# Expert layers begun from the first token tile alone, and the top-k of a head moved by half a step

## What is computed

```python
x <- LN(alpha * x + gate1 * mixer(x * (1 + scale1) + shift1))
x <- LN(alpha * x + gate2 * PEER(x * (1 + scale2) + shift2))
```

```python
q = (t @ wq).astype(f32).reshape(T, PEER_HEADS, PEER_DK)
s1 = jnp.einsum('thd,hkd->thk', q[..., :half], k1.astype(f32))
s2 = jnp.einsum('thd,hkd->thk', q[..., half:], k2.astype(f32))
v1, i1 = lax.top_k(s1, PEER_TOPK)
v2, i2 = lax.top_k(s2, PEER_TOPK)
...
top_s, pos = lax.top_k(cand_s, PEER_TOPK)
idx = jnp.take_along_axis(cand_i, pos, axis=-1)
gate = jax.nn.softmax(top_s, axis=-1)
...
act = jax.nn.gelu(jnp.einsum('td,thkd->thk', tb, u_tab[ib]).astype(f32), approximate=False)
return jnp.einsum('thk,thkd->td', (gb * act).astype(tb.dtype), v_tab[ib])
```

## Time and profile before

| what | value |
|---|---|
| median of 3 runs | 2070.34 us (2067.26 to 2072.97) |
| profiled execution | 2069.5 us |
| its span | 2067.7 us |
| TensorE busy | 1739.6 us, 84% |
| VectorE busy | 1502.9 us, 73% |
| ScalarE busy | 597.6 us, 29% |
| q0, all gathers | 536.90 MB |
| mean granted TensorE clock | 0.948 |
| gathers | 475.9 to 2038.5 us, 512 of them |

### The profile page before, as it was taken

One profiled execution on the slowest core, in us unless ns is written; L12 is line 12 of the kernel. 1 busy time (PEld: TensorE's weight loads), 2 busy tenths in 40 slices (PEclk: granted clock), 3 DMA queues, 4 the chain that ended last, 5 costly groups with the idle time before them and its releaser, 6 DMA issues.

```text
span 2067.7 us, 17872 instructions
## 1 busy us (share of the span) xinstructions
PE 1739.6 (84%) x5310; PEld 973.9 (47%) x5310; DVE 1502.9 (73%) x3506; ACT 597.6 (29%) x1415; POOL 484.1 (23%) x516
## 2 busy tenths in 40 slices
PE   5998988978899877889998899977998888777776
PEld 5777467765444332334343478654454333222222
DVE  6899986657676767888786676566767776877765
ACT  3554651512232223323232121002222222222221
POOL 0000000003333333333333000003333333333331
PEclk9999998989999999999999899988999999999999
DMA  8244216638999999899999774429999999999996
GB/s 326 89 155 144 82 62 242 248 126 348 419 420 419 420 412 417 351 402 391 383 420 380 290 295 178 167 91 419 420 420 420 417 413 412 394 419 420 420 419 258
DMA packets 94472, 668.11 MB, mean 323 GB/s; under 512 B 11271, under 2 KB 11560, under 8 KB 14504
## 3 DMA queue, kind: packets, MB, share of 16 engines
q0 software_dynamic: 73728, 536.90, 63.2%
q1 hardware_dynamic: 20648, 130.08, 16.6%
HBM read 665.82 MB, written 1.11 MB: 323 GB/s over the span
## 4 chain that ended last, share of the span: by engine, by line
PE 39%; DMA 29%; DVE 13%; issue 2%; ACT 2%; PEldq 0%; POOL 0%; PEld 0%; DVEq 0%; SPq 0%; POOLq 0%; ACTq 0%
DMA expert_rows<-in_p_uv,chosen_experts 28%; PE bank L898 21%; PE bank L965 4%; DVE dot_products L1875 4%; PE bank L864 4%; PE bank L829 2%; PE bank L808 2%; PE bank L1040 1%; PE bank L1005 1%; PE bank L994 1%; ACT weight_diagonal L1272 1%; DVE modulation_products L1395 1%; PE bank L927 1%; PE bank L915 1%; DVE scores L1839 1%
## 5 line engine op out<-in xcount | busy, mean ns | idle before, releaser
L898 PE MATMUL bank<-expert_rows,weight_diagonal 128*128 128x512 f32 x2048 | 985.0, 626 | 200.0 <-ACT weight_diagonal L1272 199.9
L1875 DVE SCALAR_TENSOR_TENSOR dot_products<-expert_rows,bank 128x1024 f32<-128x1024 f32 x512 | 624.9, 1220 | 338.3 <-DMA expert_rows<-in_p_uv,chosen_experts 332.4
L1061 POOL DMA_INDIRECT expert_rows<-in_p_uv,chosen_experts x512 | 483.9, 945 | 1555.2 <-PE bank L898 823.5
L898 PEld LDWEIGHTS bank<-expert_rows,weight_diagonal 128*128 128x128 f32 x2048 | 393.6, 198 | 730.2 <-issue 406.4
L1263 ACT ACTIVATE expert_gelu<-expert_dots 128x2 f32<-128x2 f32 x256 | 52.1, 203 | 723.2 <-DVE dot_products L1875 722.8
L1272 ACT ACTIVATE weight_diagonal<-constants,expert_weights 128x128 f32<-128x128 f32 x512 | 177.6, 394 | 228.4 <-DVE expert_weights L1813 226.4
L864 PE MATMUL bank<-t_T,weight_block 128*128 128x256 f32 x512 | 126.1, 382 | 0.9 <-issue 0.9
L864 PEld LDWEIGHTS bank<-t_T,weight_block 128*128 128x128 f32 x512 | 98.2, 193 | 50.1 <-issue 41.0
L724 PE MATMUL bank<-mixer_input_T_hi,weights_hi 128*128 128x512 f32 (+1 forms) x192 | 76.4, 398 | 25.1 <-DVE mixer_input_T_lo L1481 14.8
L965 PE MATMUL bank<-hyena_input_T,hyena_weight_block 128*128 128x256 f32 x384 | 87.1, 388 | 0.7 <-DVE hyena_input_T L1430 0.7
L1573 DVE SCALAR_TENSOR_TENSOR conv_work_or_state<-conv_work_or_state,channel_vectors 128x252 f32<-128x252 f32 (+1 forms) x192 | 82.5, 430 | 4.4
(11 more groups left out here) (256 smaller groups left out, 1863.6 us busy)
## 6 DMA issues: line engine op xcount, KB each, us to landing
weight_block<-in_ada_rows SPq DMA_DIRECT2D x24, 1024.0 KB, 4.8
weight_block<-in_m_in_blocks SPq DMA_DIRECT2D x20, 1024.0 KB, 4.9
weight_block<-in_wq_blocks SPq DMA_DIRECT2D x16, 1024.0 KB, 4.8
hyena_weight_block<-in_ada_rows SPq DMA_DIRECT2D x16, 1024.0 KB, 5.5
hyena_weight_block<-in_h_in_blocks SPq DMA_DIRECT2D x12, 1024.0 KB, 6.9
weight_block<-in_m_out_blocks SPq DMA_DIRECT2D x8, 1024.0 KB, 6.5
expert_rows<-in_p_uv,chosen_experts POOLq DMA_INDIRECT x512, 12.3
hyena_weight_block<-in_h_out_blocks SPq DMA_DIRECT2D x4, 1024.0 KB, 7.1
```

The costliest lines, as they stand in the source:

```text
L898: last = mm(ps[b][:, :], dg[n % DIAG][:, :], uv[slot][:, D + h * 512:D + (h + 1) * 512], start=(r == 0 and k == 0), stop=end)
L1061: pool.indirect_dma_start(uv[slot][:, :], None, A[f"p_uv{l}"], bass.IndirectOffsetOnAxis(ap=chosen[:, s_, k:k + 1], axis=0)).then_inc(uv_l ...
L1875: stt(prod[:, :], uv[slot][:, 0:D], 1.0, rows_t, ALU.mult, ALU.mult, accum_out=dots[:, s_, k + j:k + j + 1]).then_inc(sem("dots_done"), 1)
```

## The change

**Start of an expert part.** Only tile 0 stands ahead of choose 0: `tile_transposes` and `modulate_tile` of tile 0, `first_queries(l, 0, ...)` and `first_scores(l, 0)` for head 0 with 128 tokens. Tile 1's norm, transposes and modulation come after choose 0, then round 1 for both tiles. Head 0's queries and scores of tile 1 are made in steps 0 and 1. Rounds 2 to 7 are made in steps 0 to 5, four k of the queries behind each of a step's first four combines.

**Layer 1.** Hyena's output is made tile by tile, first all of tile 0, then tile 1 in pieces with tile 0's start between them. SP waits for bank 1 of the output (tile 0's second half), GpSimd for bank 3, instead of the barrier 3, which is gone. All four blocks of the output's weights are freed at the end of tile 1's output.

**wq.** The slot of block 0 is freed by head 0's queries of tile 1.

**Choose.** In steps 1 to 15 a step holds pieces 4 to 7 of the next step's choose in its first four pairs, and pieces 0 to 3 of the one after in its last four. Step 0 holds all of choose 1 in its third to sixth pairs, two pieces each, and pieces 0 to 3 of choose 2 in the last two. ScalarE's exponentials of the gates stand behind k = 10 of the step before.

```diff
-    stage("hout", 0, [rows("h_out_blocks", b) for b in range(4)], lambda n: by_count() if n < 3 else by_bank(("hout", 3)), hyena_ring)
-    stage(("wq", 1), 0, [columns("wq_blocks1", b) for b in range(8)], lambda n: by_bank(("q", 1, n)))
+    stage("hout", 0, [rows("h_out_blocks", b) for b in range(4)], lambda n: by_bank(("hout", 3)), hyena_ring)
+    stage(("wq", 1), 0, [columns("wq_blocks1", b) for b in range(8)], lambda n: by_bank(("q", 1, n) if n else ("q0", 1, 1)))
...
+        def tile_transposes(l, t):
+
+            pe.wait_ge(sem("layer_norms_done"), TT * 2 * l + t + 1)
+            for j in range(2):
+                b = begin(("tT", l, t, j))
+                for c in range(4):
+                    last = nc.tensor.transpose(ps[b][:, c * P:(c + 1) * P], xres[:, t, (4 * j + c) * P:(4 * j + c + 1) * P], ident)
+                last.then_inc(full[b], 1)
+
+        def first_queries(l, t, c, k0, k1):
+
+            w = block_in(pe, place[("wq", l), 0])
+            b = begin(("q0", l, t)) if c == 0 and k0 == 0 else plan(("q0", l, t))[0]
+            for k in range(k0, k1):
+                if c == 0 and k % 4 == 0:
+                    wait_read(pe, ("tT", l, t, k // 4))
+                last = mm(ps[b][:, c * P:(c + 1) * P], w[:, k * BLK + c * P:k * BLK + (c + 1) * P], tT[:, k, t * P:(t + 1) * P],
+                          start=(k == 0), stop=(k == KD - 1))
+            if c == 1 and k1 == KD:
+                last.then_inc(full[b], 1)
+
+        def first_scores(l, t):
+
+            if t == 0:
+                pe.wait_ge(sem("keys_in"), 16 * (l + 1))
+            wait_read(pe, ("q0", l, t))
+            b = begin(("sc0", l, t))
+            for a in range(2):
+                last = mm(ps[b][:, a * P:(a + 1) * P], qT[0][:, a, t * P:(t + 1) * P], kT[:, PH * a, :], start=True, stop=True)
+            last.then_inc(full[b], 1)
+
...
+        def hyena_out(t, k0, k1):
+
+            for k in range(k0, k1):
+                if t == 0:
+                    pe.wait_ge(sem("order_done"), 8 + k + 1)
+                w = block_in(pe, place["hout", k // 2])
                 for h in range(2):
...
-            for r in range(3):
-                for c in range(2):
-                    queries(r, c, 0, KD)
-                scores(r)
-                if r == 0:
-                    token_rows(0)
+            token_rows(0)
+            tile_transposes(l, 1)
+            for c in range(2):
+                queries(1, c, 0, KD)
+            scores(1)
             for s_ in range(PSTEPS):
-                r = s_ + 3
+                r = s_ + 2
                 if r == PH:
                     token_rows(1)
                 for k in range(TOPK):
                     combine(s_, k)
                     if l == 0 and s_ >= PH:
                         filter_products((s_ - PH) // 2, s_ % 2, k)
-                    if r < PH and k < 8:
-                        queries(r, k // 4, 2 * (k % 4), 2 * (k % 4) + 2)
-                    if r < PH and k == 11:
+                    if r < PH and k < 4:
+                        queries(r, k // 2, 4 * (k % 2), 4 * (k % 2) + 4)
+                    if r < PH and k == 5:
                         scores(r)
-
+                    if s_ == 0 and k >= 8:
+                        first_queries(l, 1, k // 4 - 2, 2 * (k % 4), 2 * (k % 4) + 2)
+                    if s_ == 1 and k == 6:
+                        first_scores(l, 1)
...
+        hyena_out(0, 0, KD)
+        gate_rows(1, 1)
+        hyena_out(1, 0, 4)
+        tile_transposes(1, 0)
+        hyena_out(1, 4, 6)
+        for c in range(2):
+            first_queries(1, 0, c, 0, KD)
+        hyena_out(1, 6, 7)
+        first_scores(1, 0)
+        hyena_out(1, 7, KD)
         peer(1)
...
         phase_end(pool, 2)
-        phase_end(pool, 3)
+        wait_full(pool, ("hout", 3))
...
+            copy_first_queries(0)
+            copy_first_scores(0)
+            gate_exp(0)
+            ln_root(l, 0, 1)
+            copy_queries(1)
+            copy_scores(1)
             for s_ in range(PSTEPS):
                 for k in range(0, TOPK, PAIR):
                     gelu(s_, k)
                     diagonals(s_, k)
-                    if s_ + 3 < PH and k == 8:
-                        copy_queries(s_ + 3)
-                    if s_ + 3 < PH and k == 12:
-                        copy_scores(s_ + 3)
+                    if s_ + 2 < PH and k == 4:
+                        copy_queries(s_ + 2)
+                    if s_ + 2 < PH and k == 6:
+                        copy_scores(s_ + 2)
+                    if s_ == 1 and k == 2:
+                        copy_first_queries(1)
+                    if s_ == 1 and k == 8:
+                        copy_first_scores(1)
+                    if s_ + 1 < PSTEPS and k == 10:
+                        gate_exp(s_ + 1)
...
-        layer_norm(0, 0, [("mout", j) for j in range(4)])
+        ln_stats(0, 0, 0, [("mout", j) for j in range(4)])
+        ln_finish(0, 0, 0)
         phase_end(dve, 1)
 
-        def peer(l):
-            modulate(("tT", l), tT, l, 1)
+        def peer(l, keys):
+            modulate_tile(("tT", l), tT, l, 1, 0)
...
-            for s_ in range(2):
-                for piece in range(8):
-                    choose(s_, piece)
+            for piece in range(8):
+                choose(0, piece)
+            ln_stats(l, 0, 1, keys)
+            ln_finish(l, 0, 1)
+            modulate_tile(("tT", l), tT, l, 1, 1)
...
-                    if s_ + 2 < PSTEPS:
-                        choose(s_ + 2, k // PAIR)
+                    n = k // PAIR
+                    if s_ == 0 and 2 <= n < 6:
+                        for piece in range(2):
+                            choose(1, 2 * (n - 2) + piece)
+                    elif s_ == 0 and n >= 6:
+                        for piece in range(2):
+                            choose(2, 2 * (n - 6) + piece)
+                    elif s_ and n < 4 and s_ + 1 < PSTEPS:
+                        choose(s_ + 1, 4 + n)
+                    elif s_ and n >= 4 and s_ + 2 < PSTEPS:
+                        choose(s_ + 2, n - 4)
```

More of the change, by code:

```diff
@@ L1359, in _ @@
         gate_copy(1, 1)
-        for t in range(TT):
-            ln_root(1, 0, t)
-        phase_end(act, 3)
+        ln_root(1, 0, 0)
         peer(1)
@@ L1890, in peer @@
                         dve.drain().then_inc(read[4 + 2 * t + h], 1)
-        peer(0)
+        peer(0, [("mout", j) for j in range(4)])
         for part in range(2):
```

91 lines of the change are left out of this document (36 added, 55 removed).

## The result

The changed kernel takes **2081.2 us** (median of 6 runs, 2077.43 to 2088.08) against 2070.3 before: a ratio of 1.0054, 95% interval 1.0035 to 1.0074, or 10.9 us slower.

The account below looks back on a forecast made before the run. Bound: expert gathers at the DMA rate, 2.495 us each, 639 us per layer. Layer 0 start -3.2, layer 1 start +6.7, filters -4.3, norm +1.5: a gain of 0.7, forecast 2069.0 us, range 2058 to 2080.

Parts of the forecast that it names:

- Rival C: Layer 0 filter steps: heavier choose half delays the filters, each step 8 to 14 paying 2.45, 17.2 us, about 2082; chance 0.20.
- the filters: Layer 0's steps 8, 10, 12 and 14: heavier choose piece ahead of the filters' matmuls, 4.3 us lost in all.
- the two starts: First gathers of each layer's expert part: 10.4 us of empty queue plus 3.4 of wq traffic lost in each.
- the leads: Start of each expert part: first gather 10.6 us earlier in layer 0 and 20.5 in layer 1.
- G + 20: Start of each layer's gathers: queue runs empty if gather 8 issues over 20 us after G, the first gather's issue.
- I cost them at nothing: Layer 0's odd filter steps: first half 2.45 us longer, taken as covered by 3.2 us to spare in step 11.
- the empty queue at the start: After the first gather in each layer: late gather 8, query chunks, late choose and low clock lose 10.4 us, 6 to 12.
- wq (I had 3.4): Each layer's start: all four wq blocks go among the gathers, 10 us instead of 2.5, less 4.1: 3.4 lost.
- the late choose 1: Step 0 of each layer: choose 1 ends near G + 48, late for gather 16, with gelu 6 behind a copy: 1.4 us.
- Layer 1's step 8: Tile 0's last norm stands behind lighter choose pieces 0 to 3 there: 1.5 us gained.
- The 4.1 of wq: Kernel before, layer 0: first landing 9.5 us after G, a lone gather 5.3, so 4.1 us of wq traffic ahead.
- B: Start of both expert parts: queue hardly empties, 3.5 us a layer instead of 10.4, about 2055; chance 0.27.

Follow-up runs that it names:

- e8: The changed kernel timed again without any edit: 2079.7 us, ratio 1.0043 to the kernel before.
- e4: Changed kernel with layer 1's barrier 3 back and Hyena's output over both tiles together, one-tile start kept: 2091.7 us.
- e6: Changed kernel with whole choose in layer 0's filter steps, tile 1's norm early, gelu of units 0 and 1 first, round 2's queries in chunks of two: 2052.5 us.
- e5: Changed kernel with tile 1's norm ahead of choose 0 and, in layer 1, all of Hyena's output ahead of head 0's queries: 2070.3 us.
- e1: Changed kernel with the half-step shift of choose undone in layer 0's filter steps alone: 2070.5 us, ratio 1.0004 to the kernel before.
- e9: Edit of e1: in odd steps 9, 11 and 13 choose pieces 0 to 5 stand in the first four pairs: 2076.9 us.
- e10: Edit of e1: choose piece 3 made twice in even steps 8, 10 and 12: 2071.6 us.

## Why the prediction was wrong

The forecast was no measurable change, 2069.0 in 2058 to 2080; the kernel is 10.9 us slower. The likeliest case was not the one that came. Rival C's mechanism did, with a smaller price than I gave it (9.9 to 14.1 where it had 17.2), and the starts lost more than forecast; that the time is within a microsecond of C's 2082 is a coincidence of the two. In e8, whose time is near the median, the filters are 5.6 us over their term, the two starts 6.1, the rest of layer 1 2.1 and the leads 0.2, and the mixer gave 1.5 back.

**Right.** DMA rate as the bound; the leads (10.6 and 20.5 forecast, 10.3 to 10.4 and 20.6 to 22.1 measured, with e4 putting 9 to 10 of the second on the output by tile and the barrier's end together); that an emptied queue takes them back; that gather 8 has to come by G + 20. All kernels over this bound lose 8.9 us or more at each start, and e6, under it, 5 to 6. To keep to the bound is needed, but not enough: e5 is under it too, at G + 18.6, and still loses 10, with its next gathers too far apart. Right as well: that TensorE's and ScalarE's order at the start is a part of it. The forecast's gathers 3.44 apart are there.

**The step that failed: "I cost them at nothing"**, of the odd filter steps. I took the 3.2 us to spare at the last gather of step 11 for the cover of all of them, and by my own rule it holds only while an even step hands on no more than 0.8, where my own figure was 1.0. The last gather of step 9 had 1.3 to spare, not 3.2. In step 9 VectorE waits for no landing, and in steps 11 and 13 for none from unit 6 to unit 10, before and after; TensorE and GpSimd wait for it there, so delay goes straight into gathers 14 and 15. The filters cost 9.9 to 14.1 us instead of 4.3. e1 takes the whole of it away, and e9, with 6.3 us of pieces in the first half of odd steps where the changed kernel has 5.9, shows 6.4 of it in the odd steps alone. What is left of e1's 10.7 is 4.3, which agrees with my figure for the even steps. Its mechanism is in the trace of step 8: the first filter matmul comes 3.69 us behind the start of unit 7's dot, where 2.69 stood before and stands in e1. e10 neither confirms nor excludes the price.

**Sizes that were off: the empty queue at the start**, 10.4 in each layer. Without the 3.9 of wq (I had 3.4) it was 12.4 to 14.0. Gather 8 came at G + 26.2 to 26.6, the far end of my 24.1 to 26: queries 1 began 0.8 us later than I had them and lost 2.6 us to the low clock and not 1.6 (9.65 against 7.07). The first combine and the chunk of queries behind it met a low clock once more (2.84 and 2.77 us, where later ones take 1.88 and 1.89), so the next gather came 4.3 us behind, not 3.4. The granted clock was 0.60 over the idle 458 to 473, 0.72 over 476 to 486, 0.98 over 486 to 492 and 0.50, the level of 1.2 GHz, over 492 to 494, behind a pause of TensorE from 488.0 to 490.8. The Trainium skill ("TensorE: Matmul & The Clock Gate", Part 1) has the clock fall in idle time and come back under load, and these windows agree:

```profile
458.00:473.00 15.00, 0.00 (x0) 0.00 (x0) 14.28 (x45) 2.54 (x5) 4.43 (x4) 0.60 0.24 82
476.00:486.00 10.00, 9.55 (x32) 7.80 (x32) 4.33 (x11) 0.00 (x0) 1.87 (x2) 0.72 1.00 420
486.00:492.00 6.00, 2.48 (x12) 1.71 (x12) 1.77 (x4) 3.37 (x6) 0.00 (x0) 0.98 0.77 315
492.00:494.00 2.00, 2.00 (x4) 0.88 (x4) 1.73 (x4) 0.90 (x3) 0.11 (x1) 0.50 0.02 8
```

In e6, where gather 8 is in time, 1.3 to 1.9 us remain besides wq; I put 1.4 for the late choose 1. No run tries that term by itself.

**Small.** Layer 1's step 8 was to gain 1.5; it gained 0.7 up to its last dot, and step 9 gave that back. The 4.1 of wq ahead of the first landing is 4.2 by its own numbers (9.5 less 5.3). The shortest gather from issue to landing in the changed kernel is again 5.3:

```profile
DMA to landing us min/median/max: 5.3/12.3/23.1
```

The estimate of 4.4 us for a lone gather, from the Trainium skill ("DMA: Bandwidth & Descriptors", Anatomy of one DMA — SWDGE (gpsimd) path), stays without support: 21 gathers of the changed kernel took less than 6 us, and none less than 5.3.

**The weights of the rivals.** B's 0.27 rested on TensorE reaching combine 0 in time, which TensorE's own order excluded. C's 0.20 should have been more: I wrote that it decides at 0.8 handed on, had 1.0 for that myself, and still put the odd steps at zero.
